# Two of twelve weight remainders on GpSimd in a mixture-of-experts stage

## The reference

```
gu   = rows @ w_gate_up[e] + b_gate_up[e]          # 1024 -> 2048
gate = minimum(gu[:, :1024], 7);  up = clip(gu[:, 1024:], -7, 7)
hid  = (up + 1) * (gate * sigmoid(gate * 1.702))
y    = hid @ w_down[e] + b_down[e]                  # 1024 -> 1024
```

## Time and profile before

| | |
|---|---|
| median of three executions | 2768.33 us |
| the profiled execution | 2765.02 us |
| its span | 2763.4 us |
| TensorE busy (PE) | 2537.6 us, 92% |
| VectorE busy (DVE) | 1701.2 us, 62% |
| ScalarE busy (ACT) | 1318.7 us, 48% |
| GpSimd busy (POOL) | 201.5 us, 7% |
| the 384 remainders on VectorE | 876.2 us |

### The profile page before, as it was taken

One profiled execution on the slowest core, in us unless ns is written; L12 is line 12 of the kernel. 1 busy time (PEld: TensorE's weight loads), 2 busy tenths in 40 slices (PEclk: granted clock), 3 DMA queues, 4 the chain that ended last, 5 costly groups with the idle time before them and its releaser, 6 DMA issues.

```text
span 2763.4 us, 37051 instructions
## 1 busy us (share of the span) xinstructions
PE 2537.6 (92%) x11003; PEld 1855.1 (67%) x11004; DVE 1701.2 (62%) x2447; ACT 1318.7 (48%) x1535; POOL 201.5 (7%) x188
## 2 busy tenths in 40 slices
PE   6999999868848999999999999999999999998687
PEld 3456666544426778787777878787878888777233
DVE  4653333523355796779779696768676657774354
ACT  2113333332223774658577484657564445562232
POOL 1100000001220000000000000000000000000210
PEclk9999999988868999999999999999999999999799
DMA  5009500322215896879789696869685666783541
GB/s 177 19 12 339 186 20 22 109 81 69 68 42 187 301 355 215 293 242 369 240 302 354 217 348 237 290 226 341 218 286 199 203 207 231 246 286 129 192 144 49
DMA packets 387538, 556.36 MB, mean 201 GB/s; under 512 B 18241, under 2 KB 326977, under 8 KB 387362
## 3 DMA queue, kind: packets, MB, share of 16 engines
q1 hardware_dynamic: 333922, 456.55, 49.4%
q10 hardware_dynamic: 39408, 57.67, 5.7%
q0 software_dynamic: 14160, 41.51, 4.4%
HBM read 482.91 MB, written 71.19 MB: 201 GB/s over the span
## 4 chain that ended last, share of the span: by engine, by line
PE 63%; issue 6%; DVE 6%; ACT 1%; DMA 1%; DVEq 1%; SPq 0%; ACTq 0%; POOLq 0%; POOL 0%
PE bank L554 16%; PE bank L552 16%; PE bank L553 16%; PE bank L1274 5%; PE bank L647 4%; PE bank L546 2%; PE bank L523 1%; DVE wlo L711 1%; PE bank L531 1%; PE bank L650 1%; DVE sig L732 1%; PE bank L1286 1%; DVE xlo L716 1%; DVE gat L727 0%; DVE upc L728 0%
## 5 line engine op out<-in xcount | busy, mean ns | idle before, releaser
L1458 ACT ACTIVATE whi<-raw 128x2048 fp32r<-128x2048 f32 x384 | 733.4, 1917 | 578.5 <-PE bank L554 532.2
L711 DVE TENSOR_TENSOR wlo<-raw,whi 128x2048 fp32r<-128x2048 f32 x384 | 876.2, 2286 | 210.4 <-PE bank L554 195.6
L552 PE MATMUL bank<-whi,xhi 128*128 128x512 f32 x1472 | 577.1, 392 | 0.0
L554 PE MATMUL bank<-wlo,xhi 128*128 128x512 f32 x1472 | 574.3, 390 | 0.0
L553 PE MATMUL bank<-whi,xlo 128*128 128x512 f32 x1472 | 573.8, 390 | 0.0
L554 PEld LDWEIGHTS bank<-wlo,xhi 128*128 128x128 f32 x1472 | 276.5, 188 | 58.1
L553 PEld LDWEIGHTS bank<-whi,xlo 128*128 128x128 f32 x1472 | 276.8, 188 | 57.1
L552 PEld LDWEIGHTS bank<-whi,xhi 128*128 128x128 f32 x1472 | 276.9, 188 | 54.1
L552 PE MATMUL bank<-whi,hhi 128*128 128x512 f32 x736 | 292.1, 397 | 0.0
L554 PE MATMUL bank<-wlo,hhi 128*128 128x512 f32 x736 | 287.3, 390 | 0.0
L553 PE MATMUL bank<-whi,hlo 128*128 128x512 f32 x736 | 287.0, 390 | 0.0
(11 more groups left out here) (263 smaller groups left out, 2853.6 us busy)
## 6 DMA issues: line engine op xcount, KB each, us to landing
raw<-in_w_gate_up_dram SPq DMA_DIRECT2D x512, 512.0 KB, 4.7
raw<-in_w_down_dram SPq DMA_DIRECT2D x128, 1024.0 KB, 6.9
expert_rows<-zeros ACTq DMA_DIRECT2D x1, 32768.0 KB, 103.8
expert_rows<-ysb ACTq DMA_DIRECT2D x46, 512.0 KB, 6.2
xall<-in_x_dram SPq DMA_DIRECT2D x8, 512.0 KB, 10.2
uT<-in_w_out_dram SPq DMA_DIRECT2D x1, 4096.0 KB, 14.2
xr<-in_x_dram SPq DMA_DIRECT2D x8, 512.0 KB, 6.4
h_scratch<-h SPq DMA_DIRECT2D x8, 512.0 KB, 2.8
```

What stands on the lines that cost most here:

```text
L552: pe.matmul(dst, stat_hi[:, b, kt], hi, start=False, stop=False)
L554: return pe.matmul(dst, stat_hi[:, b, kt], lo, start=False, stop=last)
L711: dve.tensor_tensor(wlo[:, c % LO], raw[:, c % RAW], whi[:, c % HI].bitcast(F32), ALU.subtract).then_inc(lo_ready, 1)
L1458: act.activation(whi[:, c % HI], raw[:, c % RAW], ACT.Copy).then_inc(hi_ready, 1)
```

## The change

GpSimd computes the remainders of pieces 3 and 9 of each item, VectorE the other ten. The one counter `lo_ready` becomes two, `lo_dve` (ten per item) and `lo_pool` (two per item), and TensorE and SyncE wait for the one that belongs to the piece. In GpSimd's program piece 3 stands before the row fetch for the next item and piece 9 after it. Its remainders wait for `hi_ready` and for `w_free` of the piece that had the wlo slot before: piece 3 for the end of the item before, piece 9 for piece 5.

```diff
+        POOL_LO = (3, 9)
+
+        def lo_wait(eng, n, c):
+            if c in POOL_LO:
+                eng.wait_ge(lo_pool, 2 * n + POOL_LO.index(c) + 1)
+            else:
+                eng.wait_ge(lo_dve, (PIECES - 2) * n + sum(q not in POOL_LO for q in range(c + 1)))
...
@@ TensorE, body
-                    pe.wait_ge(lo_ready, PIECES * n + c + 1)
+                    lo_wait(pe, n, c)
...
@@ VectorE, split_lo
-                                  ALU.subtract).then_inc(lo_ready, 1)
+                                  ALU.subtract).then_inc(lo_dve, 1)
...
@@ VectorE, before the loop and in body
             for c in range(LO):
-                split_lo(0, c)
+                if c not in POOL_LO:
+                    split_lo(0, c)
...
-                    if c + LO < PIECES:
+                    if c + LO in POOL_LO:
+                        pass
+                    elif c + LO < PIECES:
                         dve.wait_ge(w_free, PIECES * n + c + 1)
                         split_lo(n, c + LO)
...
-                        with dve.If(nxt > 0):
-                            dve.wait_ge(w_free, PIECES * n + c + 1)
-                            split_lo(n + 1, c + LO - PIECES)
+                        if c + LO - PIECES not in POOL_LO:
+                            with dve.If(nxt > 0):
+                                dve.wait_ge(w_free, PIECES * n + c + 1)
+                                split_lo(n + 1, c + LO - PIECES)
...
@@ SyncE, weight loads
-                                sp.wait_ge(lo_ready, PIECES * n + c - RAW + 1)
+                                lo_wait(sp, n, c - RAW)
                                 expert_piece(sp, e, c, c % RAW)
...
-                                    sp.wait_ge(lo_ready, PIECES * n + RAW + c + 1)
+                                    lo_wait(sp, n, RAW + c)
                                     expert_piece(sp, e2, c, c)
...
-            sp.wait_ge(lo_ready, read(sp, P - 1, BEFORE) * PIECES)
+            all_items = read(sp, P - 1, BEFORE)
+            all_dve = sp.snap(all_items * (PIECES - 2), min_val=0, max_val=MAX_ITEMS * (PIECES - 2))
+            all_pool = sp.snap(all_items * 2, min_val=0, max_val=MAX_ITEMS * 2)
+            hold(sp, lo_dve, all_dve)
+            hold(sp, lo_pool, all_pool)
...
@@ GpSimd
+            def split_lo(n, c):
+                pool.wait_ge(hi_ready, PIECES * n + c + 1)
+                pool.wait_ge(w_free, PIECES * n + c - LO + 1)
+                pool.tensor_tensor(wlo[:, c % LO], raw[:, c % RAW], whi[:, c % HI].bitcast(F32),
+                                   ALU.subtract).then_inc(lo_pool, 1)
+
             prepare(0)
...
-                        with pool.If(read(pool, n + 1, LIVE) > 0):
-                            prepare(n + 1)
+                        with pool.If(read(pool, n, LIVE) > 0):
+                            split_lo(n, POOL_LO[0])
+                            with pool.If(read(pool, n + 1, LIVE) > 0):
+                                prepare(n + 1)
+                            split_lo(n, POOL_LO[1])
```

More of the change, by code:

```diff
@@ L331, in layer @@
         hi_ready = sem("hi_ready")
-        lo_ready = sem("lo_ready")
+        lo_dve = sem("lo_dve")
+        lo_pool = sem("lo_pool")
         w_free = sem("w_free")
```

## The result

The changed kernel took 2818.35 us (median of six executions, 2808.32 to 2832.22), the kernel before beside it 2767.63 us. The ratio is 1.0192 with an interval of 1.0164 to 1.0219: 51 us slower, where 20 were forecast. The sign held, and so did the exclusion that the forecast rests on, at its forecast price in the one-block items where GpSimd starts piece 9 when the forecast says. In the ten where it starts later the loss is far larger, and the time lies outside the range of 2763 to 2812. The profiled executions took 2832.22 us (span 2830.6) and, before, 2765.02 (2763.4): 67.2 us apart in both. Counted from the first matmul of an item to that of the next, the eight one-block items with one row fetch (a one-block item follows) are 12.2 us longer in total than before, the ten with two fetches (a two-block item follows) 52.8 us, and the fourteen two-block items 1.2 us.

The account below looks back on a forecast made before the run. TensorE bounds two-block items; in one-block items VectorE, DMA and TensorE are near their end and hid ends last. 18 x 1.5 = 27 us, less 6.7, gives 20: 2785 profiled, 2788 as a median, range 2763 to 2812.

Parts of the forecast that it names:

- Exclusion: GpSimd's remainder and VectorE instructions with two SBUF inputs take turns, whole instructions at a time; stop 4.2 to 4.7 us.
- Piece 9, 1.5 us per item: In 18 one-block items GpSimd's piece 9 delays sig, hid and the turn behind piece 7 by 1.5 us: 27 us.
- Row fetch: The next item's row fetch, between pieces 3 and 9 on GpSimd, lands in time; worst case 1 us in few items.
- Piece 3, 0: GpSimd's piece 3 ends 2.3 us later, covered by VectorE's idle time and loads in flight: price 0.
- The 6.7 us given back: TensorE's 8 late matmuls in one-block items behind one-block items vanish as loads catch up: 6.7 us off the sum.
- Relief: Rival, chance 0.13: both engines read at once or share finely, VectorE gains 2 us before hid; 7 us faster, 2761.
- GpSimd first: Rival, chance 0.13: GpSimd gets the port before VectorE's piece 8 remainder, sig is 2.5 us late; 38 us, 2806.
- Covered: Rival, chance 0.13: loads bound one-block items so far that the lost time comes back; within 5 us, 2768.
- Slow restart: Rival, chance 0.04: each GpSimd change from fetch to arithmetic costs 7.6 us; 18 x 5 = 90 us, 2858.

Follow-up runs that it names:

- write-only kernel: Changed kernel with GpSimd's two remainders replaced by a zero fill of the wlo slot that reads no SBUF: 2764.09 us against 2769.93 for the kernel before.
- quarters: Changed kernel with the row fetch ahead of both remainders and each GpSimd remainder in four 128x512 instructions: 2799.89 us against 2765.59 for the kernel before.

## Why the prediction was right in part and wrong in size

*Exclusion.* Right. GpSimd's remainder alone takes 4.62 us (forecast 4.5 to 4.7) and 6.46 behind one of VectorE's (6 to 7). The port was held from 1250.65 to about 1255.06 (1251.81 + 3.67 - 0.42), 4.4 us, where 4.2 was taken. The Trainium skill's rule in "SBUF — State Buffer", section "Who interferes with whom", has a second half that the write-only kernel shows: against a GpSimd instruction that only writes, two SBUF inputs on VectorE don't matter (maximum 2294 ns).

*Piece 9, 1.5 us per item.* Right for the eight items with one fetch: the wait behind piece 7 is 1.75 us, 0.2 before and 1.55 more. With the fetch out of the way it is so in all 18 and the total is +22.5 against the forecast 20. This term stood.

*Row fetch, "at most 1 us in a few items, left to the range".* This is the step that failed. There are ten such items, not "a few": every one-block item ahead of a two-block one. The working had GpSimd's start of piece 9 near 21 us into the item as the worst case; it was 20.1 to 24.4 in these ten, with waits for the ids of up to 7.9 us where the earlier trace rows have 5.48. Then it asked only whether the piece would be ready for TensorE. It nearly always was. The question left out was whom a late start would stop, and until when. In eight items sig (seven times) or hid (once) had not run yet and stood still until GpSimd ended, at 24.7 to 27.2 us instead of 23.8: the turn behind piece 7 waits 2.8 to 5.0 us there, not 1.75. In the other two it was VectorE's next remainder, with 1.9 us at the turn within piece 9 and in one of them 1.5 us for piece 9 itself. These ten items hold 52.8 of the stage's 66.2 us. With the fetch first the loss halves (2818 and 2816 to 2792).

*Piece 3, 0.* Wrong, and more than its own +7.2 and +6.3. "Two 1 MB pieces still in flight: 0" took the DMA queue as never empty, but ScalarE's waits for loads went from 17.6 to 81.1 us with piece 3 alone. In the changed kernel such a wait stands in front of the sigmoid in each of the eight items above; that held sig back (20.2 to 22.3 us into the item, 20.1 without such a wait) and so within reach of the late piece 9. The kernel with a late piece 9 but no piece 3 had sig on time in all ten and lost 39.0 us, not 50. That both are needed for the rest is read from the traces; no run kept the late fetch and piece 3 and took only the late loads away.

*The clock.* Not in the forecast at all. The kernel before keeps a granted clock of 1.00, with no wait above 1.94 us once the stage has started. In the changed kernel it falls sixteen times behind waits of 1.8 to 5.0 us; the clock sum is 34.0 and 23.9 in the two traces and 3.4 with the fetch first. With 37.6 us more wait at the turn (46.8 against 6.7 + 2.5) that is 71.6 us for a difference of 67.2 in span; 2.7 us of the low clock lie within waits and are counted twice, and the rest of the excess isn't accounted for. So at most half of the loss is clock. That it follows from the waits is seen at every such place of the traces, but not every wait of 1.8 us is followed by it, and no run took it away by itself.

*The 6.7 us given back.* Right in the changed kernel: none of the eight late turns behind piece 3 is left. With the fetch first four of them are still there, at 0.9 to 1.2 us each, so some 4 us weren't given back, and the forecast's own sum would be 24. That the +22.5 there lies so near 20 is in part luck.

*The rivals.* Relief: with nothing stopped it is -5.8 in one place of the fetch and +4.5 in the other, where 7 us of gain was its price. GpSimd first: the item from 1231 shows VectorE's remainder of piece 8 keeping the port, as forecast; where a late piece 9 met a late sig the price was above the 2.5 us of this rival. Covered: two-block items are; one-block items aren't. Slow restart: the remainder at 1018.47, right behind a fetch, took 4.55 us, so none.

## What to carry to other kernels

Before work is moved to GpSimd, list which VectorE instructions read two SBUF tensors and which of them another engine waits for; a GpSimd instruction that reads SBUF stopped those for nearly its whole length here (4.4 of 4.6 us), and splitting it in four shortened the stop but made the piece itself later (9.3 instead of 6.5 us). Where a moved instruction can start late, ask not only whether its result is in time but what it collides with at the later start, and fix its place by an order or a wait that doesn't depend on a DMA's landing. Terms that are small alone can meet: late loads held sig back, and a late fetch then put GpSimd on it. And look first at the waits that the profile already has: one turn moved by one piece gave 23 us, where taking two remainders off an 89% busy engine, with nothing stopped, moved the time by -6 to +5.

## What the runs showed of the hardware that was not expected

- VectorE's hid was recorded from 1018.06 and GpSimd's remainder from 1018.47, yet hid took 5.26 us and GpSimd's 4.55, as undisturbed. It is so in six of the ten items with two fetches: VectorE's instruction is recorded 0.1 to 0.5 us ahead of GpSimd's and is the one that is stretched. The start in the record doesn't say who has the port.
- With quarters, VectorE gets in between GpSimd's instructions and GpSimd between VectorE's; four quarters beside a busy VectorE took 9.3 us, a whole one 6.5.
- TensorE's clock went to 0.52 in a stretch behind an idle one of nearly 5 us, and to 0.66 of full in a 5 us stretch (1295 to 1300) behind two one-block items with waits of only 1.8 us. The 1.2 and 2.4 GHz levels show as 0.43 and 0.227 us between matmuls.
